# The way into the Strassen pairs of a feed-forward layer: three steps of the vector and scalar engines in another order, and one product moved ahead

## What is computed

```python
D_MODEL = 1024
D_FF = 2816
...
    h = rms_norm(x, lp["g_ffn_pre"])
    gt, up = jnp.split(h @ lp["w_gate_up"], 2, axis=-1)
    f = (jax.nn.silu(gt) * up) @ lp["w_down"]
    x = x + rms_norm(f, lp["g_ffn_post"])
```

## Time and profile before

| what | value |
|---|---|
| median of 3 runs | 1063.36 us (1060.92 to 1064.67) |
| the profiled execution's own time | 1064.49 us |
| its span in the trace | 1062.7 us |
| granted TensorE clock, mean | 0.998 |
| PE busy | 1042.3 us (98%) |
| PEld busy | 981.7 us (92%) |
| DVE busy | 682.6 us (64%) |
| ACT busy | 503.9 us (47%) |
| POOL busy | 354.6 us (33%) |

### The profile page before, as it was taken

One profiled execution on the slowest core, in us unless ns is written; L12 is line 12 of the kernel. 1 busy time (PEld: TensorE's weight loads), 2 busy tenths in 40 slices (PEclk: granted clock), 3 DMA queues, 4 the chain that ended last, 5 costly groups with the idle time before them and its releaser, 6 DMA issues.

```text
span 1062.7 us, 26383 instructions
## 1 busy us (share of the span) xinstructions
PE 1042.3 (98%) x11199; PEld 981.7 (92%) x11199; DVE 682.6 (64%) x1184; ACT 503.9 (47%) x927; POOL 354.6 (33%) x194
## 2 busy tenths in 40 slices
PE   8999999999999999999999999998999999999998
PEld 8998899999998998999999768988999999999998
DVE  5488788788784666886470871657989989500003
ACT  6454533533533567525463534654565656522232
POOL 4431221322312410356133101452544544444450
PEclk9999999999999999999999999999999999999999
DMA  7321221221213433665144783522334333433222
GB/s 226 100 73 31 61 61 43 61 79 33 69 44 109 123 120 119 200 205 164 49 179 160 257 293 123 152 81 81 94 105 120 89 112 119 153 116 104 80 65 81
DMA packets 164061, 120.44 MB, mean 113 GB/s; under 512 B 5336, under 2 KB 153066, under 8 KB 163433
## 3 DMA queue, kind: packets, MB, share of 16 engines
q1 hardware_dynamic: 159979, 108.08, 33.0%
q10 hardware_dynamic: 3974, 10.80, 3.0%
HBM read 111.04 MB, written 8.30 MB: 112 GB/s over the span
## 4 chain that ended last, share of the span: by engine, by line
PE 84%; DVE 10%; ACT 2%; DMA 2%; issue 1%; DVEq 0%; ACTq 0%
PE ps L552 36%; PE ps L1807 16%; PE ps L1163 12%; PE ps L534 9%; PE ps L1872 3%; PE ps L574 2%; DVE conv_y L2848 2%; DVE cache L3284 1%; DMA q_bc<-q_scratch 1%; PE ps L1110 1%; DVE ps L3197 1%; PE ps L600 0%; DMA x_tok<-in_x_prompt_dram 0%; DVE m_lo L636 0%; PE ps L1100 0%
## 5 line engine op out<-in xcount | busy, mean ns | idle before, releaser
L999 POOL TENSOR_TENSOR w_lo<-w_raw,w_hi 128x1024 fp32r<-128x1024 f32 (+2 forms) x83 | 193.6, 2337 | 409.2 <-ACT w_hi L592 357.0
L552 PE MATMUL ps<-h_hi,w_hi 128*128 128x260 f32 x748 | 161.8, 298 | 0.7 <-DVE gate_b L3139 0.7
L552 PE MATMUL ps<-h_hi,w_lo 128*128 128x260 f32 x748 | 150.2, 282 | 0.0
L552 PE MATMUL ps<-h_lo,w_hi 128*128 128x260 f32 x748 | 150.2, 282 | 0.0
L592 ACT ACTIVATE w_hi<-w_raw 128x1024 fp32r<-128x1024 f32 (+2 forms) x95 | 91.2, 965 | 73.8 <-PE ps L552 61.5
L552 PEld LDWEIGHTS ps<-h_hi,w_hi 128*128 128x128 f32 x748 | 115.3, 188 | 10.3 <-issue 4.1
L552 PEld LDWEIGHTS ps<-h_hi,w_lo 128*128 128x128 f32 x748 | 115.1, 188 | 0.0
L552 PEld LDWEIGHTS ps<-h_lo,w_hi 128*128 128x128 f32 x748 | 115.1, 188 | 0.0
L2848 DVE SCALAR_TENSOR_TENSOR conv_y<-glu,prm,conv_y 128x512 f32<-128x512 f32 x120 | 104.0, 867 | 2.5
L3182 DVE TENSOR_TENSOR sq_acc<-sq_acc,sq_tmp 128x264 f32<-128x264 f32 (+2 forms) x35 | 28.7, 821 | 114.6 <-ACT sq_tmp L2707 76.0
L1050 POOL TENSOR_TENSOR w_lo<-w_raw,w_hi 128x512 fp32r<-128x512 f32 x36 | 48.3, 1341 | 104.7 <-ACT w_hi L2588 104.7
(11 more groups left out here) (569 smaller groups left out, 3081.0 us busy)
## 6 DMA issues: line engine op xcount, KB each, us to landing
w_raw<-in_w_gate_up_dram SPq DMA_DIRECT2D x44, 512.0 KB, 4.6
w_raw<-in_w_in_dram SPq DMA_DIRECT2D x38, 512.0 KB, 3.6
cache<-in_cache_mem_k_dram SPq DMA_DIRECT2D x16, 512.0 KB, 6.1
w_raw<-in_w_down_dram SPq DMA_DIRECT2D x16, 512.0 KB, 3.5
cache<-in_cache_mem_v_dram SPq DMA_DIRECT2D x14, 512.0 KB, 6.9
w_raw<-in_w_k_dram SPq DMA_DIRECT2D x8, 512.0 KB, 3.6
w_raw<-in_w_v_dram SPq DMA_DIRECT2D x8, 512.0 KB, 3.6
w_raw<-in_w_out_dram SPq DMA_DIRECT2D x8, 512.0 KB, 3.5
```

The lines of the kernel that those rows point to most:

```text
L552: mm = nc.tensor.matmul(ps[:, 2 * s + a, 0:width], w[:, k, :], x[:, x0 + k, a * width:(a + 1) * width], start=(first and k == 0 and n == 0 ...
L999: pool.tensor_tensor(lo[:, 0:kts], w_raw[:, b % RAW_SLOTS, 0:kts], hi[:, 0:kts].bitcast(F32), ALU.subtract).then_inc(w_lo_ready, 1)
```

## The change

`up_piece(1, 1)` and `up_piece(2, 1)` move ahead of three token sums and of the four low parts on DVE, `f_low(0)`, `f_low(1)` and `f_low(3)` move back, and so does the fourth weight sum of pair 1. On ACT `f_high(1)` and `gate_piece(2, 1)` go ahead of the four `t_highs`. On PE p2 of pair 0 goes directly behind p1, ahead of the wait for the token sums. No instruction is added and none removed.

```diff
     CYCLE = ("p6", "p7", "p2", "p5", "p1", "p4", "p3")
+    FIRST_CYCLE = ("p2", "p6", "p7", "p5", "p1", "p4", "p3")
...
-        at = BEFORE["product_done"] + 1 + 7 * p + CYCLE.index(name) + 1
+        at = BEFORE["product_done"] + 1 + 7 * p + (CYCLE if p else FIRST_CYCLE).index(name) + 1
...
             first_product(0)
+            second_product(0)
             pe.wait_ge(t_made, BEFORE["t_made"] + 8)
...
                 product("p7", y21_bank, True)
-                second_product(p)
+                if p:
+                    second_product(p)
...
-            t_highs(0)
-            t_highs(2)
             f_high(1)
-            t_highs(4)
-            t_highs(6)
             gate_piece(2, 1)
+            for k in range(0, KT, 2):
+                t_highs(k)
             f_high(2)
...
             up_piece(0, 1)
-            f_low(0)
             dve.wait_ge(h_summed, BEFORE["h_summed"] + 2)
             tt(tokens(0, LEFT), tokens(0, LEFT), tokens(0, RIGHT), ALU.subtract).then_inc(t_made, 1)
+            up_piece(1, 1)
             tt(tokens(0, RIGHT), tokens(0, RIGHT), tokens(4, RIGHT), ALU.subtract).then_inc(t_made, 1)
...
             tt(tokens(4, LEFT), tokens(4, LEFT), tokens(4, RIGHT), ALU.add).then_inc(t_made, 1)
-            up_piece(1, 1)
-            f_low(1)
+            up_piece(2, 1)
+            f_low(0)
             dve.wait_ge(x_moved, 16)
...
-                if k == 4:
-                    up_piece(2, 1)
+            f_low(1)
             f_low(2)
...
             sums13_low(0)
-            f_low(3)
             fourth_sum(0)
...
-                if more:
+                if more and p:
                     fourth_sum(p + 1)
...
-                dve.wait_ge(f_lo_ready, 4 + p)
+                if p:
+                    dve.wait_ge(f_lo_ready, 4 + p)
                 tt(f_banks[:, 1], p7_kept_t[:, :], chain_bank(p), ALU.subtract).then_inc(y_made, 1)
+                if p == 0:
+                    fourth_sum(1)
                 if more:
                     sums13_low(p + 1)
...
                 f_left(p)
+                if p == 0:
+                    f_low(3)
```

## The result

The changed kernel takes 1057.34 us (median of 4 runs, 1056.79 to 1058.24) where the kernel before takes 1062.97 (4 runs, 1060.92 to 1064.67): a ratio of 0.994, 95% interval 0.9925 to 0.9954, so 5 to 8 us faster, and 5.6 by the medians. The forecast was 1058.4 us, range 1055.9 to 1061.0, with 5.0 us of gain and 0.81 on faster.

What follows compares the result with a forecast made beforehand. PE, busy 98% of the span, bounds the kernel; its three waits were worth 5.17 us between starts. 5.17 - 0.15 = 5.0 us of gain takes the median from 1063.36 to 1058.4 us, range 1055.9 to 1061.0.

Steps and rivals of the forecast that it cites:

- First edit: up_piece(1, 1) behind one token sum on DVE: PE's wait ahead of B_UP+5 goes, 3.15 us and 0.08.
- the slow start: First matmul behind a PE wait takes 0.36 us instead of 0.28; 0.08 counted with the first edit's wait.
- The hold: DVE instruction with two SBUF inputs stands still until POOL's ends; first token sum held to 717.74, about 3.4 us.
- PE's cover of 2.2 us: Ahead of B_UP+5: the up product ends at 720.4, PE wants it at 722.71, 2.2 us to spare.
- Second and third edit: Pair 0: p2 behind p1 removes the wait for kept p1, 0.79 us and 0.07; y22 earlier, 1.00 and 0.08.
- What comes back: At p3 of pair 1: f_low(3) and the fourth sum stand later in DVE's list; 0.15 us charged.
- the lead: DVE's 0.8 us from the end of pair 1's y22 to p3; to shrink to between 0.5 and -0.1.
- Loads: Pair 2's blocks, asked for 3 us earlier, land in 4.6 us; nothing charged, a late load up to 1.5 us.
- DVE falls behind: Rival: extra DVE-POOL meetings in pairs 0 and 1 delay p3 of pair 1; 1059.5 or 1060.8 us; chance 0.17.
- Doesn't do what it says: Rival: B_UP+5 still waits, first sum held through both POOL splits; 1.8 us left, 1061.6 us; chance 0.07.
- slower: Rival: DVE behind PE in every pair, 0.48 us a pair to be seen, 1066.6 us; chance 0.02.

Runs made afterwards that it cites:

- only_up: Kernel before with the first edit alone (up products ahead of the token sums on DVE, ACT's list as in the change); 1059.45 us, ratio 0.9961.
- up_behind_t3: Changed kernel with the up product of tile 1 two sums later on DVE, behind the third token sum; 1058.90 us.
- low3_again: Changed kernel with f_low(3) at the end of pair 3's list and pair 2's fourth sum behind pair 1's y22; 1056.47 us.
- only_p2: Kernel before with only p2 of pair 0 moved directly behind p1; 1063.98 us, ratio 0.9991.
- up_as_before: Changed kernel with DVE's old order up to up_piece(1, 1), f_low(0) again behind the first up product; 1062.20 us.
- after_again: The changed kernel unaltered, measured once more on another chip; 1058.25 us, kernel before 1063.57.
- before_look: The kernel before unaltered, profiled once more to see the clock behind the 3.0 us wait; 1065.66 us (one run).

## Why the prediction was right

**First edit.** Forecast 3.15 us and 0.08 for the slow start; only_up measures 3.24. The times of the forecast, moved by the 1.45 us of the earlier arrival, are met to 0.1 us: the up product at 720.0 (718.56 + 1.45 = 720.01), B_UP+5 at 722.7 (722.71), p1 at 737.1 (737.11). The hold passed to the first sum as worked out (3.41 us for 3.4), and PE's cover of 2.2 us was real: up_behind_t3 went beyond it, and B_UP+5 began 1.27 us late (a listed wait of 1.10).

**Second and third edit.** The end of the two together was right (p3 of pair 0 at 747.2, measured 745.71 + 1.45 = 747.16; y22 ended at 744.54, 1.2 us ahead of it, the upper end of the 0.4 to 1.2 forecast), the split between them was not: I wrote 0.79 us for p2 ahead and 1.00 for y22 as if each stood alone. p2 ahead alone is worth nothing, since DVE's list sets p3 of pair 0, 11.95 us behind the end of the blocks, whatever PE does meanwhile. The third edit's step in the prediction had this number; the second's did not use it.

**What comes back.** This is the term that was mis-sized: 0.15 us charged, and 5.17 - 4.81 = 0.36 measured. The row is the one ahead of p3 of pair 1, at 756.09: 0.15 us of idle, and p3 to p3 takes 10.38 us instead of 10.07. DVE's rows of the changed kernel that lead to it:

```profile
751.26 1.71 DVE L3418 TENSOR_TENSOR h_lo<-sum_tmp,h_hi 128x512 fp32r<-128x512 f32 x1
752.90 1.77 DVE L3413 TENSOR_TENSOR h_lo<-sum_tmp,h_hi 128x512 fp32r<-128x512 f32 x1
754.59 0.42 DVE L3476 TENSOR_TENSOR ps<-ps,p_kept_t 128x260 f32<-128x260 f32 x1
754.93 0.68 DVE L3404 TENSOR_TENSOR sum_tmp<-sum_tmp,w_raw 128x512 f32<-128x512 f32 x1
755.53 0.42 DVE L3483 TENSOR_TENSOR ps<-p_kept_t,ps 128x260 f32<-128x260 f32 x1
```

with POOL's:

```profile
751.12 1.30 POOL L1051 TENSOR_TENSOR zg_lo<-w_raw,zg_hi 128x512 fp32r<-128x512 f32 x1
752.38 1.74 POOL L1051 TENSOR_TENSOR w_lo<-w_raw,w_hi 128x512 fp32r<-128x512 f32 x1
```

Two low parts in a row are held, 1.71 and 1.77 us instead of 0.69. But holds alone did not eat the lead, for there were two in the kernel before as well. From the end of y22 of pair 0 to that of pair 1 DVE now takes 755.95 - 744.54 = 11.41 us, before 761.59 - 752.14 = 9.45. Of the 1.96 us more, counted by starts, 1.03 are the fourth sum of pair 1, now behind the first y22, and 0.60 are `f_low(3)`; the two low parts cost 2.13 more, against 1.04 less at `gate_sums(2)` (1.22 instead of 2.27 us) and 0.77 less at the fourth sum of pair 2 (0.68 instead of 1.45). Measured from the start of B_UP+4, y22 of pair 1 moved ahead by 41.78 - 37.59 = 4.19 us, and the prediction had 4.3 to 4.9: its interval for the lead, 0.5 to -0.1, should have gone to -0.2.

**Loads.** I charged nothing, and that needs a word. The chain that ended last, in the changed kernel, runs through the load of pair 2's blocks:

```profile
742.79 0.37 SPq L929
743.16 0.05 issue
743.21 4.83 DMA w_raw<-in_w_gate_up_dram
```

It landed at 748.04, and ACT waited 0.60 us for it, which put POOL's splits later. But in low3_again ACT waits 0.56 us for the same load and PE waits for nothing. So the load takes part in the timing of the holds, and less work on DVE ahead of y22 is enough to end the wait in spite of it. What an earlier load would bring was not tried.

**The size.** The rows give 4.81 us, the medians 5.6 and 5.3. The median of 1057.34 us lies 1.1 under the forecast; the kernel before, measured along with it, came out 0.4 under its earlier median. The rest fits a slow clock that the first profile did not show behind the wait of 3 us: it was there in four profiles of five, at 1.4 to 2.7 us, and behind B_UP+5 in none of the nine others of the table. The mean granted clock that is on record for each execution points the same way. It averages 0.9973 over 84 executions of kernels with the wait of 3 us (before, only_p2, up_as_before) and 0.9984 over 54 of kernels with a wait of 1.1 us or none there. As an estimate, 0.0011 of 1060 us are up to 1.2 us for an execution on average (less where the clock was low while PE waited); for the kernel before and after_again on one chip, 0.9970 and 0.9978, it is up to 0.8. That is of the size of what is left, but within the scatter of these runs (1056.18 to 1063.91 for after_again), and a mean doesn't say where the clock was low. It also bounds the chance: the smallest fall seen, 3 us at 0.50, makes a mean of 0.998, and 8 of the 84 have 1.000, so at least these did not fall. up_as_before, 3.95 us slower than after_again where the wait and its slow start are worth 3.2, agrees; the share of the executions that fall stays open.

**The rivals.** "DVE falls behind" happened in small, as the term above: 0.36 us instead of 1.3. "Doesn't do what it says" and "slower" did not: behind p3 of pair 1 the PE of the changed kernel runs without a wait to the end of the pairs.

## What to carry to other kernels

A helper engine that works through its list in order has a pace of its own: where that list sets when a result comes, moving the consumer's other work around gains nothing, and two edits that meet there must be priced together. Look first for the small instruction that frees a bank and stands behind long ones that nobody waits for yet; here one product of 0.42 us, moved past three sums and a low part, was worth 3.2 of 4.8 us. Measure such edits by the distance between two starts that enclose them, since spans of two executions differed by 1.45 us ahead of the change.

## What the runs showed of the hardware

The clock behind a pause of this length differs from one execution to the next. With the same wait of 2.96 to 2.99 us ahead of B_UP+5 the granted clock behind it was 1.00 once and 0.50 four times, for about 3 us in three profiles and for about 7 us in before_look, at 1.4 to 2.7 us each; the slow stretch began between 0.8 us ahead of PE's restart and 0.9 us behind it. Behind waits of 1.10 and 2.37 us it stayed at 1.00, in one profile each. But 2.37 us is not a safe length. The first profile of the kernel before has one more long wait, 2.12 us in the attention, and a slow stretch of some 3 us that begins 0.9 us behind it:

```profile
624.52 0.39 PE L1685 MATMUL ps<-ident,sc 128*16 128x128 f32 x2 [2.12 <-DVE h_lo L3273]
...
625.66 0.42 PE L534 MATMUL ps<-h_lo,wx_hi 128*128 128x256 f32 x1
```

A matmul of 0.28 us takes 0.42 there. Between 16 and 1050 us of all 14 profiles the clock fell only behind or in such waits, one of 2.12 us and four of 2.96 or 2.99; waits of 1.4 to 1.7 us (1.38, 1.70, 1.71) had no fall behind them. The Trainium skill agrees in kind: TensorE: Matmul & The Clock Gate, section Why this matters for your kernels, warns of idle gaps between bursts of matmuls as what brings the lower clock back. What the profile of one execution shows of such a wait can therefore be its lower price.

DVE and POOL hold each other for whole instructions, and what a held instruction costs is set by when it asks: the same second sum took 3.44 us before, 1.86 in the changed kernel and 3.43 in up_behind_t3, against 1.23 for a sum of the same size unheld. Each time it ended 1.1 us behind POOL's instruction (722.82 and 721.72, 720.77 and 719.67, 719.85 and 718.76). SBUF — State Buffer in the Trainium skill, section Who interferes with whom, says this of two SBUF inputs and of who issues first, and the rows bear it out; instructions with one input in PSUM took their 0.42 us beside a working POOL.
